# The opening of a hybrid decoder step: the first pool group takes weights before the running mean, and TensorE spreads the norm's weight row

## The reference

```
u   = x * rsqrt(mean(x*x) + 1e-6) * norm_mix          # per token
for group g with window w in (2, 4, 8, 16), 512 features each:
    pooled = running mean of u over the last w tokens # samples continue from a buffer of 15 old tokens
    d      = pooled - u
    y[g]   = d @ pool_w[g]                            # 512 x 512
h   = x + y * pool_scale
```

## Time and profile before

| | before |
|---|---|
| median of 3 runs | 2434.45 us (2433.37 to 2435.29) |
| the profiled execution's own time | 2432.01 us |
| its span | 2430.3 us |
| TensorE busy | 2410.8 us (99%) |
| VectorE, ScalarE, GpSimd busy | 1158.5, 877.0, 506.9 us |
| granted TensorE clock, mean | 0.999 |

### The profile page before, as it was taken

One profiled execution on the slowest core, in us unless ns is written; L12 is line 12 of the kernel. 1 busy time (PEld: TensorE's weight loads), 2 busy tenths in 40 slices (PEclk: granted clock), 3 DMA queues, 4 the chain that ended last, 5 costly groups with the idle time before them and its releaser, 6 DMA issues. The chain is left out here.

```text
span 2430.3 us, 43060 instructions
## 1 busy us (share of the span) xinstructions
PE 2410.8 (99%) x16236; PEld 2364.6 (97%) x16236; DVE 1158.5 (48%) x1332; ACT 877.0 (36%) x1048; POOL 506.9 (21%) x624
## 2 busy tenths in 40 slices
PE   9999999999999999999999999999999999999998
PEld 9999999999999999999987799999999999999997
DVE  6644444444444454544467775443344344434354
ACT  6333233233323333322445454332333233323332
POOL 7520022012101332210322113320022012101321
PEclk9999999999999999999999999999999999999999
DMA  6544444444444444555587764544454455445443
GB/s 236 176 149 153 148 147 150 152 148 147 150 151 147 147 146 142 148 151 148 168 275 251 243 191 147 150 153 147 148 151 151 147 148 151 150 147 149 145 155 109
DMA packets 198695, 389.69 MB, mean 160 GB/s; under 512 B 12229, under 2 KB 12485, under 8 KB 198153
## 3 DMA queue, kind: packets, MB, share of 16 engines
q1 hardware_dynamic: 197664, 385.78, 51.3%
q0 software_dynamic: 960, 2.94, 0.4%
HBM read 366.47 MB, written 22.66 MB: 160 GB/s over the span
## 5 line engine op out<-in xcount | busy, mean ns | idle before, releaser
L1108 DVE TENSOR_TENSOR w_lo<-w_raw,w_hi 128x1024 fp32r<-128x1024 f32 x648 | 826.5, 1277 | 1177.8 <-ACT w_hi L791 1161.4
L791 ACT ACTIVATE w_hi<-w_raw 128x1024 fp32r<-128x1024 f32 x608 | 644.7, 1061 | 1302.3 <-PE G L1590 1274.0
L1588 PE MATMUL G<-op_hi,w_hi 128*128 128x320 f32 x2816 | 873.3, 310 | 2.4 <-DVE qkv L1504 2.4
L1589 PE MATMUL G<-op_lo,w_hi 128*128 128x320 f32 x2816 | 868.2, 308 | 0.0
L1590 PE MATMUL G<-op_hi,w_lo 128*128 128x320 f32 x2816 | 868.2, 308 | 0.0
L1588 PE MATMUL G<-a_hi,w_hi 128*128 128x320 f32 x2304 | 711.1, 309 | 2.1 <-DVE hT L1227 0.8
L1589 PE MATMUL G<-a_lo,w_hi 128*128 128x320 f32 x2304 | 710.1, 308 | 0.0
L1590 PE MATMUL G<-a_hi,w_lo 128*128 128x320 f32 x2304 | 710.1, 308 | 0.0
L1588 PEld LDWEIGHTS G<-op_hi,w_hi 128*128 128x128 f32 x2816 | 528.1, 188 | 6.6 <-issue 4.6
L1589 PEld LDWEIGHTS G<-op_lo,w_hi 128*128 128x128 f32 x2816 | 528.1, 188 | 2.4 <-issue 1.0
L1590 PEld LDWEIGHTS G<-op_hi,w_lo 128*128 128x128 f32 x2816 | 528.0, 188 | 0.0
(11 more groups left out here) (253 smaller groups left out, 886.8 us busy)
## 6 DMA issues: line engine op xcount, KB each, us to landing
w_raw<-in_ffn_w_up SPq DMA_DIRECT2D x256, 512.0 KB, 3.7
w_raw<-in_ffn_w_down SPq DMA_DIRECT2D x256, 512.0 KB, 3.8
w_raw<-in_mlstm_w_in SPq DMA_DIRECT2D x96, 512.0 KB, 3.9
w_raw<-in_mlstm_w_out SPq DMA_DIRECT2D x32, 512.0 KB, 4.4
cst<-in_state_mlstm_C SPq DMA_DIRECT2D x26, 512.0 KB, 4.2
out_C_sample<-cst SPq DMA_DIRECT2D x26, 512.0 KB, 3.4
w_raw<-in_pool_w SPq DMA_DIRECT2D x8, 512.0 KB, 11.4
w_raw<-in_state_mlstm_C SPq DMA_DIRECT2D x6, 512.0 KB, 3.7
```

The costliest lines, as they stand in the source:

```text
L791: act.activation(w_hi[:, c % RING], w_raw[:, c % RING], ACT.Copy).then_inc(w_hi_ok, 1)
L1108: v.tensor_tensor(w_lo[:, slot], w_raw[:, slot], w_hi[:, slot].bitcast(F32), ALU.subtract).then_inc(w_lo_ok, 1)
L1588: pe.matmul(G[:, m, 0:T], w_hi[:, slot, t, w], hi[:, k, :], start=first and t == 0, stop=False)
L1589: pe.matmul(G[:, m, 0:T], w_hi[:, slot, t, w], lo[:, k, :], start=False, stop=False)
```

## The change

Group 0 is computed in the other order. Its 512 raw features of the 320 new tokens, times the norm's weights, and those of the 56 old tokens of a new input, `near`, are split (`xs_hi`, `xs_lo`), and TensorE multiplies them by both weight chunks with tokens on the output's partitions (`features_first`, 36 matmuls of 512 columns into three banks of G). ScalarE and VectorE copy the three banks out, times the token's scale (`z_out` and its VectorE twin), and TensorE applies `band` to the result (`pooled_prompt`, `pooled_samples`), which lands in G where `pooled` takes it. Groups 1 to 3 keep their way, but group 1's differences are now made between `pooled_prompt(2)` and `pooled_prompt(3)`, and VectorE scales the band of group 1 instead of that of group 0. The 1 MB load of the weight row is replaced by a load of 8 KB to one partition, four matmuls with a column of ones into X0 to X3, and four copies to `gain`. The order of loads changes, the residuals of groups 2 and 3 go behind pool chunks 5 and 7, and `samples(0)`, now needed only for an output, goes to the feed-forward. Semaphores, tile declarations and adapted counts are left out of the cut below.

```diff
-WARM = (13, 5, 8, 6)
+WARM = (22, 4)
+FIRST = (1, 2, 3, 0)
 TURN = (1, 0, 2, 3)
+XS = TP + NS + NSEQ * NEAR
+SPARE = 8
+Z_BANK = (0, 1, 3)
 SQ_RING = 6
...
+        near = yT[:, 10, 0:MT * NSEQ * NEAR].rearrange("p (k r) -> p k r", r=NSEQ * NEAR)
+        z_rows = yT[:, 11:16, :].rearrange("p a t -> p (a t)")[:, 0:TT * NC].rearrange("p (t n) -> p t n", n=NC)
+        xs_hi, xs_lo = (x[:, SPARE:SPARE + MT + 1, :].rearrange("p a t -> p (a t)")[:, 0:MT * XS].rearrange("p (k r) -> p k r", r=XS)
+                        for x in (a_hi, a_lo))
+        gain_row = junk[0:1, :]
...
-            for t in range(TT):
+            def row_load(t):
                 src = A["x_prompt"][0, t * P:(t + 1) * P, :] if t < 2 else A["sample_rows"]
                 sp.dma_start(xrow[:, t, :], src).then_inc(x_in[t], 16)
-            sp.dma_start(gain[:, 0:NC], A["mix_rows"][:, 0:NC]).then_inc(gain_in[0], 16)
+
+            sp.dma_start(gain_row, A["norm_mix"][0:1, :]).then_inc(row_in, 16)
+            pool_load(0)
             sp.dma_start(vecs[:, :], A["vec_cols"]).then_inc(vecs_in, 16)
-            pool_load(0)
+            residual_load(0)
+            sp.dma_start(near, A["near_cols"]).then_inc(near_in, 16)
+            row_load(0)
             pool_load(1)
-            residual_load(0)
-            sp.dma_start(gain[:, NC:], A["mix_rows"][:, NC:]).then_inc(gain_in[1], 16)
+            row_load(1)
+            row_load(2)
             pool_load(2)
             pool_load(3)
             residual_load(1)
             sp.dma_start(far[0:NS, :], A["state_far"]).then_inc(far_in, 16)
-            residual_load(2)
-            residual_load(3)
...
+                if n % 2:
+                    residual_load(n // 2)
...
             draw(0)
-            for g in range(1, GROUPS):
+            draw(1)
+            for g in range(2, GROUPS):
                 draw(g)
...
+            def xs_split(k):
+
+                act.activation(xs_hi[:, k, 0:T], hT[:, k, :], ACT.Copy, scale=vec(V_MIX + k)).then_inc(xs_hi_ok, 1)
+
+            def z_out(t):
+
+                rows = slice(0, XS - TP if t == 2 else P)
+                act.wait_ge(z_ok, t + 1)
+                act.wait_ge(r0_ok, t + 1)
+                act.activation(z_rows[rows, t, :], G[rows, Z_BANK[t], :], ACT.Copy, scale=rcol[rows, t:t + 1]).then_inc(z_act, 1)
+
+            for n in range(2):
+                act.wait_ge(gain_wide, n + 1)
+                act.activation(gain[:, n * NC:(n + 1) * NC], X[n][:, :], ACT.Copy).then_inc(gain_act, 1)
+            split_pool(0)
+            act.wait_ge(vecs_in, 16)
+            act.wait_ge(h_in[0], 16)
+            xs_split(0)
+            xs_split(1)
+            act.wait_ge(near_in, 16)
+            act.activation(xs_hi[:, :, T:], near, ACT.Copy).then_inc(xs_hi_ok, 1)
+            xs_split(2)
+            xs_split(3)
             square(0)
+            split_pool(1)
             tile_root(0)
             square(1)
             tile_root(1)
             square(2)
-            act.wait_ge(vecs_in, 16)
-            d_hi(0, 1)
+            z_out(0)
             tile_root(2)
-            split_pool(0)
-            for i in TURN[1:]:
-                d_hi(0, i)
-            split_pool(1)
-            for g in range(GROUPS + 1):
+            z_out(2)
+            split_pool(2)
+            for i in FIRST:
+                d_hi(1, i)
+            split_pool(3)
+            for g in range(1, GROUPS + 1):
...
+            def xs_split(k):
+
+                v.wait_ge(xs_hi_ok, (1, 2, 4, 5)[k])
+                v.scalar_tensor_tensor(out=xs_lo[:, k, 0:T], in0=hT[:, k, :], scalar=vec(V_MIX + k),
+                                       in1=xs_hi[:, k, 0:T].bitcast(F32), op0=ALU.mult, op1=ALU.subtract).then_inc(xs_lo_ok, 1)
...
+            for n in range(2, 4):
+                v.wait_ge(gain_wide, n + 1)
+                v.tensor_copy(gain[:, n * NC:(n + 1) * NC], X[n][:, :]).then_inc(gain_dve, 1)
+            v.wait_ge(vecs_in, 16)
+            v.wait_ge(h_in[0], 16)
+            xs_split(0)
+            xs_split(1)
+            v.wait_ge(xs_hi_ok, 3)
+            v.tensor_tensor(xs_lo[:, :, T:], near, xs_hi[:, :, T:].bitcast(F32), ALU.subtract).then_inc(xs_lo_ok, 1)
+            split_pool(0)
+            xs_split(2)
+            xs_split(3)
             half_square(0)
             tile_inverse(0)
-            v.wait_ge(band_drawn, 1)
-            rooted(0)
+            split_pool(1)
             half_square(1)
             tile_inverse(1)
-            rooted(1)
             half_square(2)
             tile_inverse(2)
+            v.wait_ge(band_drawn, 2)
+            rooted(0)
+            rooted(1)
+            v.wait_ge(z_ok, 2)
+            v.tensor_scalar(z_rows[:, 1, :], G[:, Z_BANK[1], :], rcol[:, 1:2], None, ALU.mult).then_inc(z_dve, 1)
 
             def samples(g):
 
                 cols = slice(g * NC, (g + 1) * NC)
                 x = xrow[0:NS, 2, cols]
-                v.wait_ge(gain_in[1 if g else 0], 16)
+                v.wait_ge(gain_act, 2)
+                v.wait_ge(gain_dve, 2)
                 v.scalar_tensor_tensor(out=x, in0=x, scalar=rcol[0:NS, 2:3], in1=gain[0:NS, cols], op0=ALU.mult,
                                        op1=ALU.mult).then_inc(u_ok, 1)
 
             v.wait_ge(r0_ok, 3)
-            samples(0)
-            v.wait_ge(vecs_in, 16)
-            d_lo(0, 1)
-            split_pool(0)
-            for i in TURN[1:]:
-                d_lo(0, i)
             samples(1)
...
+            for i in FIRST[:-1]:
+                d_lo(1, i)
+            split_pool(2)
+            pooled(0)
+            d_lo(1, 0)
+            samples(2)
+            for g in range(1, GROUPS):
+                if g > 1:
                     pooled(g - 1)
                 split_pool(2 * g + 1)
-                if g < 2:
-                    samples(g + 2)
+                if g == 1:
+                    samples(3)
...
-                    pe.matmul(G[:, 0, 0:P], ident[:, :], ident[:, :], start=True, stop=True)
+                    pe.matmul(G[:, 2, 0:P], ident[:, :], ident[:, :], start=True, stop=True)
 
             pe.wait_ge(consts, 1)
             keep_warm(9)
+            pe.wait_ge(row_in, 16)
+            for n in range(4):
+                pe.matmul(X[n][:, :], one[0:1, 0:1].broadcast_to([1, P]), gain_row[:, n * NC:(n + 1) * NC], start=True,
+                          stop=True).then_inc(gain_wide, 1)
+            keep_warm(WARM[0])
+
+            def features_first(c):
+
+                pe.wait_ge(w_hi_ok, c + 1)
+                for n, (w, x) in enumerate(((w_hi, xs_hi), (w_hi, xs_lo), (w_lo, xs_hi))):
+                    if n == 2:
+                        pe.wait_ge(w_lo_ok, c + 1)
+                    for i in range(CK):
+                        k = CK * c + i
+                        if n < 2:
+                            pe.wait_ge(xs_lo_ok if n else xs_hi_ok, (1, 2, 4, 5)[k])
+                        for t in range(TT):
+                            if t == 2 and n < 2 and c == 0:
+                                pe.wait_ge(xs_lo_ok if n else xs_hi_ok, 3)
+                            at = slice(t * P, t * P + P if t < 2 else XS)
+                            ins = pe.matmul(G[0:at.stop - at.start, Z_BANK[t], :], x[:, k, at], w[:, c, i, :], start=n == k == 0,
+                                            stop=n == 2 and k == MT - 1)
+                            if n == 2 and k == MT - 1:
+                                ins.then_inc(z_ok, 1)
+                if c == 0:
+                    ins.then_inc(gemm, 1)
+
+            for c in range(2):
+                features_first(c)
+            keep_warm(WARM[1])
...
+            def pooled_prompt(m):
+
+                w = slice(m * P, (m + 1) * P)
+                pe.matmul(G[:, m, 0:BT], z_rows[:, 0, w], band[:, 0, B0:B0 + BT], start=True, stop=False, skip_group_check=True)
+                pe.matmul(G[:, m, P:TP], z_rows[:, 1, w], band[:, 0, B1:B1 + P], start=False, stop=True, skip_group_check=True)
+
+            def pooled_samples(m):
+
+                rows = slice(0, NS + NSEQ * NEAR)
+                pe.matmul(G[:, m, TP:T], z_rows[rows, 2, m * P:(m + 1) * P], band[rows, 0, BS:BP], start=False, stop=True,
+                          skip_group_check=True).then_inc(gemm, 1)
...
-            keep_warm(WARM[0])
-            pe.wait_ge(x_in[0], 16)
-            pe.wait_ge(band0_ok, 1)
-            for i in range(MT):
-                prompt(0, i, 0)
-            keep_warm(WARM[1])
-            pe.wait_ge(x_in[1], 16)
-            pe.wait_ge(band0_ok, 2)
-            for i in (1, 2, 3, 0):
-                ins = prompt(0, i, 1)
+            pe.wait_ge(band_drawn, 1)
+            pe.wait_ge(z_act, 1)
+            pe.wait_ge(z_dve, 1)
+            for m in range(MT - 1):
+                pooled_prompt(m)
+            for t in range(TT):
+                pe.wait_ge(x_in[t], 16)
+            pe.wait_ge(gain_act, 2)
+            pe.wait_ge(gain_dve, 2)
+            pe.wait_ge(band1_ok, 2)
```

(64 more changed lines are left out.)

1 line of the change is left out of this document (removed).

## The result

The changed kernel takes **2444.22 us** in the median of 6 runs (2442.31 to 2446.65), against 2434.51 (2433.37 to 2436.56) in 6 runs of the kernel before: ratio 1.0041, 95% interval 1.0028 to 1.0053. It is slower by 9.7 us, where 3.2 were forecast and 2441.5 was the upper end of the range.

A forecast was written before the change was run, and what follows sets the result against it. TensorE was taken to bound the kernel: chunk 2 starts 4.2 us later (31.7 against 27.53), less 1.0 us regained before chunk 4, net +3.2 on 2434.45, giving 2437.6 us. The range ran from 2433.0 to 2441.5 us.

The forecast's parts named there:

- the price of the spreading matmuls: TensorE's opening: first spread 1.4 us, three more 0.86 each, ending at 9.7; 22 identities of 4.9 then end at 14.6.
- The bounds 0.86 and 1.72: Time in us of one spreading matmul of 512 columns: 0.86 at the high clock, 1.72 all at the low clock.
- rival B: Slow spreading matmuls in the opening: clock stays low through them and rises 4.8 us later; net +8.4, 2442.8 us; chance 0.13.
- T: Theory tested in the experiments, rival B of the prediction: matmuls with one contracting row do not bring TensorE's clock up.
- R: Rival theory in the experiments: the clock rose late for a reason unrelated to the rows, chance included; no chance stated.
- T0: The point where group 0's band products start on TensorE, forecast at 23.9 us.
- The products' pace: Group 0's 36 matmuls of 512 columns at 0.234 us each, 8.4 us in all, ending at 23.0.
- the wait of 2.1 us on `a_lo`: New TensorE idle before chunk 2, waiting for VectorE; forecast at about 2.3 us.
- VectorE ready before the products' end: VectorE's band scalings done at 21.2, bank copy possible by 21.9, but waiting for the product at 22.8.
- the wait before chunk 4: TensorE's 1.0 us lost to VectorE's eviction before chunk 4; forecast to go, making +4.2 a net +3.2.
- Rival A: VectorE's chain sets T0, which can fall to 21.9, not lower; +1.2, 2435.7 us; chance 0.16.
- Rival C: GpSimd slows VectorE's splits and `w_lo` in the opening: T0 26.1, net +5.4, 2439.9 us; chance 0.06.

The follow-up runs named there:

- e2: Changed kernel with the four one-row spreads behind 22 identities and 9 identities after them, instead of 9 before and 22 after; 2440.84 us, ratio 1.0026 to the kernel before.
- e3: Changed kernel without the 22 identities behind the spreads; 2439.32 us, ratio 1.0016 to the kernel before.
- e7: Kernel before plus only the 8 KB row load, four one-row spreads and copies, with 2 identities behind them instead of 13; 2439.62 us, ratio 1.003.
- e10: The changed kernel itself, unaltered, run again for a third profile; its one run took 2443.37 us.
- e4: Changed kernel with nine identity matmuls into X3 filling the wait before chunk 2; 2442.78 us, ratio 1.0032 to the kernel before.
- e9: The changed kernel itself, unaltered, run again for a second profile; 2442.65 us, ratio 1.0035 to the kernel before.
- e1: Changed kernel with the four spreads replaced by identity matmuls of 128 contracting rows, so the weight row does not reach gain; one run, 2437.41 us.
- e5: Changed kernel with the weight row spread by 128 contracting rows (cleared tile, repeated identity column), same results; 2437.62 us, ratio 1.0024 to the kernel before.
- e6: Kernel before plus only group 0's new order, without spreads or their copies, gain loaded by a broadcasting transfer; 2436.08 us, ratio 1.0011.
- e8: As e6, with samples(1) before the last band products, d_lo(1, 0) before pooled(0), and four identities as fill; 2433.31 us, ratio 0.9997 to the kernel before.

## Why the prediction was wrong

**The step that failed** is the price of the spreading matmuls: "I take the clock's rise where it was, at 6.7: the first costs 1.4, three more 0.86, end 9.7", and with it "22 identities, 44 x 0.111 = 4.9: 14.6". The bounds 0.86 and 1.72 were nearly right: the three profiles of the kernel have 1.78, 1.78 and 0.96, so two lie at the upper one, and the 1.7 each that the prediction named as a sign of being wrong came. Measured, the spreads end at 13.17 instead of 9.7 and the identities at 20.09 instead of 14.6. Wrong was the reason for the lower one: that the array is busy all the time was my argument against rival B, and busy is not what the clock followed. The one-row spreads fill TensorE's time, and in every profile that has them a stretch at the low level during or behind them costs time (behind them in e2, e3, e7 and e10; after the change, in e4 and in e9 the rise came only in the identities that follow). In the profiles with 128 rows in the same place (e1, e5) there is none: the clock rose within the four and stayed up. That is seven profiles against two, and the medians of the change and of e5 go the same way. That is T, shown for this place in this kernel; R would need an execution with quick spreads and no fall, and there was none. How many rows between 1 and 128 are enough was not tried. The first product is late by 1.6 us in one of the two cases and by 5.5 in the other.

Rival B was right in mechanism and in detail: with 1.72 each and a rise 4.8 us behind the spreads (12.6 + 4.8 = 17.4), it had the fills' end at 19.8, T0 at 29.1 and 2442.8 us; measured are a rise at about 17.4, 20.09, 29.45 and 2444.22. What it lacks is the fall in chunk 2. Its chance of 0.13 was too small. The range should have reached it: between the two ends of an unknown price I drew its edge short of the far one.

The Trainium skill, "TensorE: Matmul & The Clock Gate", Part 1, says that a hardware block sets the clock "based on how busy the PE has been recently". The runs agree in direction, but a reader who takes busy as the share of time with a matmul in the array is misled: here that share was full.

**What held.** The products' pace (8.4 us) and all steps from T0: chunk 2 at T0 + 7.8 in the changed kernel, e5, e6 and e1; the wait of 2.1 us on `a_lo`; VectorE ready before the products' end. e5, the change with the clock held, was forecast to 0.1 us at chunk 2, and its feed-forward starts 3.5 later than before (61.02 against 57.56) for 3.2 forecast; 0.3 of that is the wait before chunk 4, which I had let vanish. That its median is the forecast's 2437.6 is in part luck, since its runs fall in two groups and the median is the top of the lower; it is 4.0 over the kernel before on the same chip. Rival A's floor for T0, 21.9, was passed by e6 and e8 (20.55 and 20.50) only because without spreads VectorE starts at 8, not 12. Rival C found little support: operand splits in the opening took 0.5 each, and a `w_lo` of 1.75 in e5 cost nothing, as VectorE still had to wait 1.7 us for the products.

**The parts.** They are read best from the start of the feed-forward, since all kernels have nearly the same work behind it. Against 57.56 before, the new order alone is 0.2 later (e6). The spreads as such, in TensorE's queue and ahead of VectorE's and ScalarE's first work, add 3.3 (e5 less e6). The one contracting row adds 7.1 in the slow case (68.17 less 61.02, of which 1.6 are the fall in chunk 2) and 3.2 in the quick one (e10). The medians split the 9 to 10 us otherwise: 2.5, 1.5 and 4.7 to 5.7. But each of them is known only to some 2.4 to 3.5 us either way, so they show only that the one row is the largest part; the 2.5 of the new order in particular does not stand in its opening.

**Not foreseen and open** is the fall of the clock in chunk 2, 1.6 us. It stands in all five profiles that have one-row spreads and an unfilled wait, and in none of the three with that wait but without them (e1, e5, e6); with the wait filled it came later, with (e4) or without (e8) one-row spreads. Both follow stretches of weak work, an idle one or the small differences of group 3. Neither suffices: the same idle passed without a fall in three profiles, and the same differences did in all but two. The two groups also differ in when the clock had last risen, about 6.5 to 6.8 in e1, e5 and e6 and 12.8 to 17.4 in the five, so the spreads need not be the cause; what decides whether the fall comes was not settled.

## What to carry to other kernels

A matmul that spreads one row over the partitions kept TensorE busy here but its clock low, and let a raised clock fall: if it must stand near a start, give it all 128 rows (a selector times a cleared tile), or load the row by DMA where the queue has room. Spreads, and identities put in as fills, are work in the queue: without the spreads (e5 to e6) the first product moved from 14.5 to 11.2, and all 3.3 us came through to the feed-forward; without the 22 identities (e10 to e3) it was 3.2. And before an order is turned round, count what stood in waits for free: half of the 5.4 us of differences did (group 0's), and after the change all such work stands on the path, with the 2.1 us wait behind it. That is why e6, whose first product starts 6.4 us ahead of the 17.61 of the earlier trace rows, starts its feed-forward no earlier.

## What the runs showed of the hardware that was not expected

- Four float32 matmuls of 512 columns and one row took 7.1 us or 3.9 us in executions of the same kernel, depending on whether the clock rose as they began (e10) or only in the identities behind them (the first profile, e9); the 18 identity records before them took the same 4.2 us in both.
- The granted clock reads 1.00 in the stretch in which these matmuls run at half pace for the first time, and is lower (0.83, 0.86) only where a clock that was up goes down. The start of a kernel has to be read from the pace of its records.
- The stretches at the low level behind one-row matmuls are seen both in identities (e2, 3.5 us for 18 records) and in the products themselves (e3, 2.9 for six).
